# Attention in a two-layer encoder: the next head's preparation placed on other steps of the current head, and half products issued ahead of a step's turnings

## The reference, cut to what matters

```python
c_q, c_kv, k_rope = split(u @ w_in, [384, 640])
q = (rmsnorm(c_q, q_norm) @ w_q_up).reshape(b, L, 16, 96)
kv = (rmsnorm(c_kv, kv_norm) @ w_kv_up).reshape(b, L, 16, 64 + 64)
k_nope, v = split(kv, [64])
k = concat([k_nope, broadcast(k_rope)])
q, k = rope(rmsnorm(q, q_head_norm)), rope(rmsnorm(k, k_head_norm))
s = einsum('bqhd,bkhd->bhqk', q, k) / sqrt(96)
o = einsum('bhqk,bkhd->bqhd', softmax(s), v)
h = h + o.reshape(b, L, 16 * 64) @ w_out
```

## Time and profile before

| | us |
|---|---|
| median of 3 runs | 3034.85 (3023.1 to 3037.23) |
| profiled execution: its own time | 3033.28 |
| its span | 3031.1 |
| granted clock of TensorE over the span | 0.981 |
| attention loop, first S to last T | about 122.5 to 629 |

### The profile page before, as it was taken

The page is one execution under the profiler, slowest core; times in us unless marked ns, Lnnn a source line. Parts: engine busy times, 40 slices in busy tenths (PEclk is TensorE's granted clock), DMA queues, the critical chain, the costliest instruction groups (busy, mean ns, idle before and its releaser), DMA issues.

```text
span 3031.1 us, 47789 instructions
## 1 busy us (share of the span) xinstructions
PE 2935.4 (97%) x18181; PEld 2645.1 (87%) x18181; DVE 1885.8 (62%) x2962; ACT 1187.5 (39%) x2060; POOL 1764.8 (58%) x1122
## 2 busy tenths in 40 slices
PE   8999999899999999999999999999999999999998
PEld 8999989889999999999999988677777788888776
DVE  6566766655534346777788851677778834445666
ACT  4466666632333334553111122222323433334552
POOL 4434554443777777765444443467674577776774
PEclk9989999999999999999999999999999999999999
DMA  3011110121222335442333423332323233335442
GB/s 128 26 37 34 44 34 24 43 93 42 85 88 93 106 100 167 143 136 70 97 115 91 138 86 118 119 122 96 124 94 120 65 108 101 100 102 171 147 134 91
DMA packets 200167, 290.44 MB, mean 96 GB/s; under 512 B 17159, under 2 KB 109319, under 8 KB 199943
## 3 DMA queue, kind: packets, MB, share of 16 engines
q1 hardware_dynamic: 160338, 240.07, 24.5%
q10 hardware_dynamic: 39605, 47.34, 4.7%
HBM read 212.43 MB, written 74.92 MB: 95 GB/s over the span
## 4 chain that ended last, share of the span: by engine, by line
PE 76%; DVE 8%; POOL 7%; issue 4%; DMA 2%; ACT 2%; SPq 1%; POOLq 0%; DVEq 0%; ACTq 0%
PE PS L1420 73%; PE PS L1671 2%; DMA Wraw<-in_w 1%; POOL Wlo L1256 1%; POOL Wlo L1316 1%; DVE PR L3163 1%; PE PS L2031 1%; POOL SQ L1361 1%; SPq L974 0%; DVE GD L3787 0%; POOL RMS L1326 0%; POOL Wraw L1274 0%; POOL Wraw L1272 0%; PE PS L2183 0%; DVE KR L3054 0%
## 5 line engine op out<-in xcount | busy, mean ns | idle before, releaser
L1420 PE MATMUL PS<-Uhi,Whi 128*128 128x352 f32 (+2 forms) x2028 | 514.0, 329 | 16.3 <-DVE Ulo L2948 13.7
L1420 PE MATMUL PS<-Uhi,Wlo 128*128 128x352 f32 (+2 forms) x2028 | 509.2, 327 | 0.0
L1420 PE MATMUL PS<-Ulo,Whi 128*128 128x352 f32 (+2 forms) x2028 | 508.0, 326 | 0.0
L1256 POOL TENSOR_TENSOR Wlo<-Wraw,Whi 128x512 fp32r<-128x512 f32 x242 | 329.7, 1366 | 133.5 <-ACT Whi L2591 133.3
L1132 POOL TENSOR_TENSOR Whi<-Wraw,const 128x1024 fp32r<-128x1024 f32 x64 | 159.1, 2486 | 423.0 <-PE PS L1420 408.1
L1420 PEld LDWEIGHTS PS<-Uhi,Whi 128*128 128x128 f32 x2028 | 342.2, 190 | 38.8 <-issue 15.6
L1420 PEld LDWEIGHTS PS<-Uhi,Wlo 128*128 128x128 f32 x2028 | 345.2, 189 | 19.4
L1420 PEld LDWEIGHTS PS<-Ulo,Whi 128*128 128x128 f32 x2028 | 344.0, 189 | 20.1
L2591 ACT ACTIVATE Whi<-Wraw 128x512 fp32r<-128x512 f32 x242 | 151.3, 629 | 330.7 <-POOL Wraw L1274 137.1
L1420 PE MATMUL PS<-T,Whi 128*128 128x264 f32 (+1 forms) x1328 | 219.0, 288 | 2.1 <-DVE H L3471 1.9
L1420 PEld LDWEIGHTS PS<-T,Whi 128*128 128x128 f32 x1328 | 186.4, 188 | 3.1 <-DVE H L3471 2.4
(11 more groups left out here) (449 smaller groups left out, 7432.8 us busy)
## 6 DMA issues: line engine op xcount, KB each, us to landing
Wraw<-in_w SPq DMA_DIRECT2D x192, 256.0 KB, 2.9
Wraw<-in_w SPq DMA_DIRECT2D x91, 512.0 KB, 3.9
Wraw<-in_w SPq DMA_DIRECT2D x168, 128.0 KB, 2.7
xt<-XTT ACTq DMA_DIRECT2D x20, 640.0 KB, 5.7
opd<-HID SPq DMA_DIRECT2D x40, 264.0 KB, 3.4
T<-opd SPq DMA_DIRECT2D x18, 528.0 KB, 4.3
Ulo<-opd SPq DMA_DIRECT2D x17, 528.0 KB, 4.9
Ulo<-opd SPq DMA_DIRECT2D x17, 512.0 KB, 5.3
```

What stands on the lines that cost most here:

```text
L1256: pool.tensor_tensor(f.oplo[j % SLOTS], FIRST_S2 if (p, k) == (0, 6) else f.factors[k], f.ophi[j % SLOTS].bitcast(F32), ALU.subtract).then ...
L1420: ins = pe.matmul(out, lhsT, rhs, start=start, stop=stop, skip_group_check=True)
```

## The change

On TensorE P moves from steps 0 to 3 (10, 8, 10, 8 matmuls) to steps 0 to 2 (18, 10, 8), both halves of the query norms from steps 4 and 5 to step 3, K from steps 6 and 7 to 5 and 7, V from four pieces at steps 6 to 9 (2, 2, 2 and 4 blocks) to five pieces of 2 blocks at steps 5 to 9; O is issued in front of T(n-1) and not behind it. ScalarE's `take_q` goes from steps 2 and 4 to 1 and 3, HV from 3 to 2, HQ from 6 to 5, `take_k` from 7 and 8 to 6 and 8, W to step 4 of every head that has one. VectorE's Q0 and Q1 go from steps 6 and 7 to 4 and 5, its `take_k` to 6 and 8. The chain has 12 operations and not 14: factors that were multiplied in are folded into the operands ahead of the loop. On GpSimd LW stands behind `turn_queries` in every head, and `scale_outputs` at the end.

```diff
-V_PARTS = ((0, 2), (2, 4), (4, 6), (6, KW))
+V_PARTS = tuple((w, w + 2) for w in range(0, KW, 2))
...
-            if j % 2 and split_unit(j) is not None:
-                low_weights(j)
-            if j >= 4 and j % 2 == 0:
-                scale_outputs(j // 2 - 2)
             turn_queries(nxt)
-            if j % 2 == 0 and split_unit(j) is not None:
+            if split_unit(j) is not None:
                 low_weights(j)
             if nxt % 2 == 0:
                 scale_keys(nxt)
...
+            if j >= 4 and j % 2 == 0:
+                scale_outputs(j // 2 - 2)
...
                 scores(t)
+                if half_at_turn(t):
+                    outputs(*half_at_turn(t))
                 if t >= 1:
                     turn_probs(t - 1)
-                if half_at_turn(t):
-                    outputs(*half_at_turn(t))
...
-                    if n < 4:
-                        project_q(nxt, n // 2, n % 2)
-                    if 4 <= n < 6:
-                        query_norms(nxt, n - 4)
-                    if nxt % 4 == 0 and n >= 6:
-                        project_v(nxt // 4, n - 6)
+                    if n == 0:
+                        project_q(nxt, 0, 0)
+                        project_q(nxt, 0, 1)
+                    if n in (1, 2):
+                        project_q(nxt, 1, n - 1)
+                    if n == 3:
+                        query_norms(nxt, 0)
+                        query_norms(nxt, 1)
+                    if nxt % 4 == 0 and n >= 5:
+                        project_v(nxt // 4, n - 5)
                     if nxt % 2 and nxt + 1 < HEADS:
-                        if 6 <= n < 8:
-                            project_k((nxt + 1) // 2, n - 6)
+                        if n in (5, 7):
+                            project_k((nxt + 1) // 2, n // 7)
...
-                    if n in (2, 4):
-                        take_q(nxt, n // 2 - 1)
-                    if nxt % 2 and nxt + 1 < HEADS and 7 <= n < 9:
-                        take_k((nxt + 1) // 2, n - 7)
+                    if n in (1, 3):
+                        take_q(nxt, n // 3)
+                    if nxt % 2 and nxt + 1 < HEADS and n in (6, 8):
+                        take_k((nxt + 1) // 2, n // 8)
...
-                    if n == 3 and nxt % 4:
+                    if n == 2 and nxt % 4:
                         high_values(nxt)
-                    if n == 6:
+                    if n == 5:
                         high_q(nxt)
...
-                if j >= 0 and split_unit(j) is not None and n == (1 if j % 2 else 4):
+                if j >= 0 and split_unit(j) is not None and n == 4:
                     high_weights(j)
...
-                vec.tensor_tensor(v, part_sum(A_STAT, 0), tok(K_A2), ALU.mult).then_inc(stats_taken, 1)
+                vec.tensor_tensor(v, part_sum(A_STAT, 0), tok(K_A2), ALU.add).then_inc(stats_taken, 1)
                 vec.wait_ge(stats_taken, STATS["q", x] + 1)
-                step(vec.tensor_scalar(v, v, EPS, None, ALU.add))
...
-            chain_round(y, v, a, y)
-            chain_round(y, v, a, v)
-            vec.scalar_tensor_tensor(y, v, -1.0 / math.sqrt(QK), tok(K_A), ALU.mult, ALU.mult).then_inc(qs_ready, 1)
+            chain_round(y, v, a)
+            chain_product(y, v, a)
+            vec.scalar_tensor_tensor(y, a, 1.5, y, ALU.add, ALU.mult).then_inc(qs_ready, 1)
...
-                if nxt < HEADS and nxt % 4 == 0 and n >= 7:
-                    take_v(nxt // 4, n - 7)
+                if nxt < HEADS and nxt % 4 == 0 and n >= 6:
+                    take_v(nxt // 4, n - 6)
...
-                if nxt % 2 and nxt + 1 < HEADS and 7 <= n < 9:
-                    take_k((nxt + 1) // 2, n - 7)
+                if nxt % 2 and nxt + 1 < HEADS and n in (6, 8):
+                    take_k((nxt + 1) // 2, n // 8)
...
-                    if n in (6, 7):
-                        query_factors(nxt, n == 7)
+                    if n in (4, 5):
+                        query_factors(nxt, n == 5)
```

More of the change, by code:

```diff
@@ L102 @@
 TURN_FIRST = 3
+Q_FIRST = 5
 CHAIN_V, CHAIN_A = 128, 160
@@ L1565, in project_q @@
                     wait_prep("q", x, s)
-                project(pair(bank), s, of, range(KQ), 0, 5)
+                project(pair(bank), s, of, range(KQ), 0, Q_FIRST)
                 return
-            project(pair(bank), s, of, range(KQ), 5).then_inc(prep_full, 1)
+            project(pair(bank), s, of, range(KQ), Q_FIRST).then_inc(prep_full, 1)
             if x % 2 and s:
@@ L1725, in _ @@
         project_v(0, 3)
+        pe.wait_ge(prep_taken, PREP["v", 0, 0] + 1)
+        project_v(0, 4, 6)
         for j in range(HEADS):
@@ L3020, in _ @@
                 step(vec.tensor_tensor(tok(dst), tok(dst), tok(K_R1), ALU.mult))
-                step(vec.scalar_tensor_tensor(tok(dst2), tok(dst), 1.0 / QK, tok(dst), ALU.mult, ALU.mult))
+                step(vec.scalar_tensor_tensor(tok(dst2), tok(dst), 1.0 if k else 1.0 / (QK * EPS), tok(dst), ALU.mult, ALU.mult))
+                step(vec.reciprocal(tok(dst2), tok(dst2)))
         step(vec.tensor_copy(tok(K_BV), tok(K_B)))
@@ L3072, in chain, with chain_seed, chain_product, chain_round @@
             return ap if n == 1 else ap.rearrange("p (k w) -> p k w", w=KW)
-        def chain_seed(y, v, a):
+        def chain_seed(y, v, a, sign):
             step(vec.tensor_scalar(a.bitcast(I32), v.bitcast(I32), 1, None, ALU.logical_shift_right))
-            step(vec.tensor_scalar(y.bitcast(I32), a.bitcast(I32), -1.0, float(0x5F3759DF), ALU.mult, ALU.add))
-        def chain_round(y, v, a, out):
+            step(vec.tensor_scalar(y.bitcast(I32), a.bitcast(I32), -1.0, float(0x5F3759DF - (sign < 0) * 2**31), ALU.mult, ALU.add))
+        def chain_product(y, v, a):
             step(vec.tensor_tensor(a, v, y, ALU.mult))
             step(vec.scalar_tensor_tensor(a, a, -0.5, y, ALU.mult, ALU.mult))
-            step(vec.scalar_tensor_tensor(out, a, 1.5, y, ALU.add, ALU.mult))
+        def chain_round(y, v, a):
+            chain_product(y, v, a)
+            step(vec.scalar_tensor_tensor(y, a, 1.5, y, ALU.add, ALU.mult))
         def key_factors(p, part):
@@ L3089, in key_factors @@
                 vec.wait_ge(stats_full, STATS["k", p] + 1)
-                vec.tensor_tensor(v, part_sum(A_STAT, 0, 2), pairwise(K_B2), ALU.mult).then_inc(stats_taken, 1)
+                vec.scalar_tensor_tensor(v, part_sum(A_STAT, 0, 2), 1.0 / QK, pairwise(K_RR), ALU.mult, ALU.add)\
+                    .then_inc(stats_taken, 1)
                 vec.wait_ge(stats_taken, STATS["k", p] + 1)
-                step(vec.tensor_tensor(v, v, pairwise(K_RR), ALU.add))
-                chain_seed(y, v, a)
-                chain_round(y, v, a, y)
+                chain_seed(y, v, a, 1)
+                chain_round(y, v, a)
                 return
-            chain_round(y, v, a, y)
-            chain_round(y, v, a, v)
+            chain_round(y, v, a)
+            chain_product(y, v, a)
             if p:
                 vec.wait_ge(stats_full, STATS["t", p - 1] + 1)
-            vec.tensor_tensor(KS[:], v, pairwise(K_B), ALU.mult).then_inc(ks_ready, 1)
+            vec.scalar_tensor_tensor(KS[:], a, 1.5, y, ALU.add, ALU.mult).then_inc(ks_ready, 1)
         def query_factors(x, part):
@@ L3106, in query_factors @@
                 vec.wait_ge(stats_full, STATS["q", x] + 1)
[L3107 removed]
+                vec.tensor_tensor(v, part_sum(A_STAT, 0), tok(K_A2), ALU.add).then_inc(stats_taken, 1)
                 vec.wait_ge(stats_taken, STATS["q", x] + 1)
[L3109 removed]
                 if x >= 2:
                     vec.wait_ge(p_full, (x - 1) * PER_HEAD)
[L3112 to L3113 removed]
+                chain_seed(y, v, a, -1)
+                chain_round(y, v, a)
                 return
[L3115 to L3117 removed]
+            chain_round(y, v, a)
+            chain_product(y, v, a)
+            vec.scalar_tensor_tensor(y, a, 1.5, y, ALU.add, ALU.mult).then_inc(qs_ready, 1)
         def turn_first_queries():
@@ L3205, in _ @@
         vec.sem_inc(row_ready, 1)
-        step(vec.tensor_scalar(tok(K_RR), tok(K_RR), EPS, None, ALU.add))
+        step(vec.scalar_tensor_tensor(tok(K_RR), tok(K_RR), EPS, tok(K_B2), ALU.add, ALU.mult))
         key_factors(0, 0)
@@ L3220, in _ @@
         take_v(0, 3)
+        take_v(0, 4, 6)
         for j in range(HEADS):
```

## The result

The changed kernel takes 3106.04 us (median of 4, 3103.22 to 3112.75), the kernel before 3033.47 beside it: a ratio of 1.0258, with a 95% interval of 1.0236 to 1.028. That is 72.6 us slower. The profiled execution took 3103.2 us, its span is 3101.4, 70.3 above the span before.

The account below looks back on a forecast made before the run. TensorE bounds the attention, with waits from three other streams. Four heads: 110.9 + 26.7 waits + 8.2 half clock = 145.8 us, 16.2 more; fifteen heads 61, the last about 2: 3096, median 3098 us, range 3070 to 3125.

Parts of the forecast that it names:

- Step 6: O(6) waits for VectorE's add: 3.2 us in kind 2 behind `take_k`, 1.7 in kind 1, 2.25 in kind 3.
- Step 3: N's second half waits for ScalarE's `take_q` square: 0.85 us, 1.05 with a key chain in the head, 0.35 without HV.
- O in front of T: On TensorE T(n-1) comes 1.31 us later; without filler, 0.85 us of waiting at T(4) and, without V, at T(6).
- Waits and clock: Four heads' attention: 26.7 us of waits against 10.5 before, and today's half clock, 8.2 us, kept.
- rival D: Clock lost more: each head falls at step 3 and step 6, twice today's or more; 3129 us and above, chance 0.12.
- A: Rival, faster: the waits in steps 4 to 6 don't arise, freed steps 6 to 9 carry through; 3008 us, chance 0.17.
- B: Rival, no change: new waits fall where the clock would be half, half of them hidden; about 3035 us, chance 0.14.
- C: Rival, clock kept: no half clock in the loop while the waits come as summed; 3067 us, chance 0.17.
- GpSimd's floor for kind 1: GpSimd's work behind LW keeps the next head's S(0) from coming before about 30.4 us, above today's 29.0.
- The shorter chain: VectorE's chain has two fewer operations a head: 0.4 us where the chain is waited for.
- GpSimd's order: `scale_outputs` leaves the place before the low weights: 2.4 us gained in kind 0, but `high_values` moves back by as much.

Follow-up runs that it names:

- x1: The changed kernel with the half products of the outputs (O) back behind the step's turnings (T), all else as changed: 3033.0 us, ratio to before 0.9998.
- x4: The kernel before with only the half products of the outputs put in front of the step's turnings: 3065.0 us, ratio 1.0098.
- x8: The changed kernel with nineteen matmuls a head that nobody reads, placed where TensorE waits: 3068.2 us, ratio 1.0121.
- x5: The changed kernel with half products behind the turnings, the add in front of VectorE's `take_k`, the second half of query norms in step 4: 3026.9 us, ratio 0.9988.
- x6: The kernel before with the chain of 12 operations alone, at its old steps 6 and 7: 3021.4 us, ratio 0.9969.
- x10: The kernel before with chain of 12, GpSimd's new order, second `take_k` behind step 8's maximum, odd heads' second chain part cut in two: 2995.2 us, ratio 0.9877.

## Why the prediction held, point by point

- **Step 6, the dearest place: right.** 3.2 us of waiting were worked out for kind 2, and TensorE was idle for 3.12; 1.7 for kind 1 (from start to start 470.07 less 467.72 less S's 0.8: 1.55), 2.25 for kind 3 (1.93 idle), S(6) 1.3 (1.12 idle). The path by OB, HQ, square, `take_k`, add is the one in the rows. In kind 0 K waited 2.7 us for low weights (3.0 predicted) and O(6) 0.74 (1.3): at half clock S(6) itself was longer. The path to K's wait was another than the one worked out. GpSimd was free at 426.98, 17.9 us into the head and earlier than the 18.5 of the prediction, and then idle for 1.22 us until ScalarE's W was done, which stands behind HT(3) and exp(4); the prediction took W to be beside other work:

```profile
427.08 1.04 ACT L2468 ACTIVATE Whi<-Wraw 128x1024 fp32r<-128x1024 f32 x1
...
428.20 2.35 POOL L1212 TENSOR_TENSOR Wlo<-Wraw,Whi 128x1024 fp32r<-128x1024 f32 x1 [1.22 <-ACT Whi L2468]
```

- **Step 3, N behind the square: right in kinds 0 to 2, a third too large**, 0.5 to 0.7 us idle in heads 8 to 10 against 0.85 to 1.05; in kind 3 nothing against 0.35.
- **O in front of T: the mechanism right, its waits about right, its price in clock left out.** The sum gave it 0.85 us at two places of a head, T(4) and T(6). At these places, and at T(9), the four heads wait for 2.1 us and not for 6.8. Yet undoing the order (x1) takes 1.8 us a head from TensorE's idle time, and imposing it on the old layout (x4) adds as much. The balance lies in step 6: O ahead of T holds T until the add is there, and what follows comes late; in x1 O(6) of head 10 waits 2.06 us and not 3.12. The prediction had this delay in its times for step 6, under other names. The larger part of x1's 73 us is clock, for which the sum had no term; in x4 the order cost no clock.
- **Waits and clock: the sum right, its split wrong.** Predicted: 26.7 us of waits and 8.2 of clock in four heads. Measured, by the heads' clock above: clock 0.17 x 39.5 + 0.05 x 31.8 + 0.13 x 38.5 + 0.09 x 36.6 = 16.6, so waits 146.4 - 110.9 - 16.6 = 18.9. The clock lost twice as much as today's, which was rival D's premise, and the waits less, since where the clock is half, S and O fill what would have been a wait (T(6) waited 0.2 us or less and not 0.85; in x8, at full clock, it waits 0.56). That the two errors, 8 us each in four heads, cancelled in 146.4 against 145.8 is luck.
- **The rivals.** A and B fall with the result, C with the clock at 0.89. A named what would have made it true, fewer new waits than 10.5; there were 18.9. GpSimd's floor for kind 1, 30.4 us, was never reached by the changed kernel (31.8); x1 and x5 got to 30.4 and 28.7, so the floor was too high: it moves with W, and W with TensorE's steps.
- **The shorter chain: too cheap.** It was put at 0.4 us where waited for; x6 shows 10 us over the loop, most of it clock (35 to 25). GpSimd's order: 2.4 us a head of kind 0 was counted as won and as lost again to HV's later start. K's wait of 2.7 us agrees with no gain being left, though W had a part in it, as above; on the old layout the order wins 8.

## What to carry to other kernels

Where one operand chain closes a loop (here scores, maximum, exponential, turning), what is put in front of the next link on an in-order engine delays it by its length and by every wait it brings along. Here ten matmuls, 1.31 us, at four places of a head cost 1.8 us of waits a head and not 5.2, since part is hidden; in the old layout, which has filler at more of these places, it was 1.9. So put ready work behind the link. Before moving an operation into a step, look which wait of that same step stands behind it on its new engine's queue. And a wait can cost twice when TensorE is the bound: once as time, and once for what it does to the clock. It need not: x4 has 28 us more of waits than the kernel before and no more half clock. The fillers of x8 tell the two apart cheaply.

## What the runs showed of the hardware

Work that nobody reads made the kernel faster: 285 matmuls more in the loop (4015 records against 3729), a mean clock of 0.96 and not 0.89, and 38 us less. In the kernel before, the clock stood at half, 1.2 GHz, in the earlier trace rows with TensorE busy all the stretch long; what had come before it was a wait of 0.47 us, the matmuls of K, S and T, sums of two columns, and a wait of 0.79:

```profile
406.80 0.48 PE L1420 MATMUL PS<-Chi,Whi 128*128 128x264 f32 x2 [0.47 <-DVE KR L3054]
...
409.63 1.06 PE L1420 MATMUL PS<-const,SQ 128*106 128x2 f32 x10
411.48 0.49 PE L1420 MATMUL PS<-KHI,QHI 128*106 128x264 f32 x2 [0.79 <-DVE PR L3163]
```

In x10 all four kinds of head stand at 1.00. It has fewer waits (5.7 us idle in heads 8 to 11, and 7.9 before), but not none of that size: at the end of head 9 it still waits for 1.09 and 1.24 us, at 412.55 and 416.56. So no one length of wait marks the fall in these traces, and which of the waits and narrow sums brings it about no run separates. The Trainium skill names long idle gaps as what to avoid (TensorE: Matmul & The Clock Gate, HAM oscillation — how this bites in real kernels). The rows here show the clock fall after waits much shorter than those of that section, and x8 shows that filling such waits kept it up in three kinds of head.
